# Output projection of the second token tile: one pass over both column halves in place of two

## The chip, the cores and the metric

One core of a Trainium2 chip runs the whole kernel. The metric is the device time of one execution in microseconds (us). Work is spread over five engines that run their own instruction streams and meet at semaphores: TensorE (PE, with its weight loads shown apart as PEld), VectorE (DVE), ScalarE (ACT), GpSimd (POOL) and SyncE (SP), whose queue issues nearly all DMAs here.

## What is computed

One encoder layer on 256 tokens of width 1024, in float32: two attention mixers, gated and merged, one output projection with a residual add, then a top-4-of-32 mixture of experts and a final norm. The change lies between the merged attention and the experts.

```python
def reference(x, norm1_g, w_in, ..., w_o, norm2_g, w_router, b_router, w_gate_up, b_gate_up, w_down, b_down, final_g):
    for l in range(DEPTH):
        ...
        merged = gate_a * (o_a @ w_a_out[l]) + gate_b * (o_b @ w_b_out[l])
        x = x + merged @ w_o[l]
        h2 = rmsnorm(x, norm2_g[l])
        x = x + moe(h2, w_router[l], b_router[l], w_gate_up[l], b_gate_up[l], w_down[l], b_down[l])
    return rmsnorm(x, final_g)
```

`moe` takes the four highest router logits of each token, softmaxes them, sends the token to those experts (`act = (up + 1) * gate * sigmoid(1.702 * gate)`, then `@ w_down`) and sums the weighted results. The experts' weights are 32 x 12 MB, so about 400 of the 434 MB that the kernel reads.

## The kernel before

**Tiles and stages.** The 256 tokens are two tiles of 128 (`t` = 0, 1). The width of 1024 is eight `k` tiles of 128, and results come in two column halves of 512 (`n` = 0, 1), each one PSUM bank. All weights pass through `ring`, 24 slots of 1 MB in SBUF. The front's weights (input projection, attention, `wo`) use slots 0 to 15; slots 16 to 23 are work space of the front until the experts need them. One expert takes 12 slots (8 of `in_up`, 4 of `in_down`), so the ring holds two experts, which the code calls one turn; there are 16 turns, 0 to 15. Turns 0, 1 and 15 are loaded slot by slot (1 MB each, L392), turns 2 to 14 in groups of four slots (4 MB each, L424).

**What lets a load go.** All these loads are issued by SP in program order. The loads of front slots and experts wait on `freed`, a count that PE raises when it has read a slot for the last time. Of turn 0 the loads into slots 7, 8, 9 and 10 wait for the four slots of `wo` (counts 24 to 27), the load into slot 21 is right behind them, the load into slot 22 waits for the router's logits of both tiles (`logit_done`, since it overwrites `x2T`), and that into slot 23 for `sums_opened` and the fourth `h2_ready` (it overwrites `xrow`). Turn 1's load into slot s waits until expert 0 or 1 has used slot s. So SP's queue, around the change, is: slots 7, 8, 9, 10, 21, 22, 23 of turn 0, then turn 1 from slot 0.

**The work around the change**, all of it in an order written out by hand:

- PE: `project(t, k, n)` (L1305) multiplies the merged tile `gateT[:, k, t]` by half n of row tile k of `wo`. Tile 0 runs k outside, n inside. Tile 1 runs all k for n = 0, then all k for n = 1 (L1334 to L1358), with other work placed between: `turn_rows(t, j)` (L1285, four transposes of half j of the new rows of tile t), `route(t, ks)` (L1299, router logits), L1350 (counts), `gather_first` (L1321, gathers tokens for experts 0 and 1). After the second pass come `turn_last_rows` (L1293, the last half in two quarters), the rest of `route(1)`, counts and gathers, and then expert 0 (L1415: up and gate, L1429: down).
- DVE: `residual(t, n)` (L874) adds a projection bank to `xrow`; `take_x2T` (L879) and `take_last_x2T` (L884) copy transposes out; `choose(t)` (L896 to L907) finds the top four of a tile; `normed` (L911) writes `h2`; `first_picks(t)` (L921 to L927) makes the gather masks of experts 0 and 1. `residual(1, 0)` waits for `wo_done` 2, the end of the first pass; `residual(1, 1)` waits for the end of the second.
- ACT: squares for the norm (L626), copies (L636, L631), exponentials (L649), and `take_xT` (L659), the last copy before expert 0.

Counts in the views are of machine instructions: one float32 matmul call of L1305, L1299, L1321, L1415 is two, a transpose is one.

Of the kernel before, what the change touches and what calls it, by code (L numbers as in the profile page):

```python
# [31 lines left out]
SEQ = 256  # L32
TT = SEQ // P
KT = D // P
# [115 lines left out]
def build(nc, x, x_cols, norm2_g, w_router, b_router, b_gate_up, b_down, final_g,  # L150
# [5 lines left out]
    with ExitStack() as ctx:  # L156
# [117 lines left out]
        freed = sem("ring_freed")  # L274
# [18 lines left out]
        wo_done = sem("wo_done")  # L293
        x2_ready, x2_sq, h2_ready = sem("x2_ready"), sem("x2_squares"), sem("h2_ready")
        x2T_ps, x2T_v, x2T_a = sem("x2T_ps"), sem("x2T_vector"), sem("x2T_scalar")
# [33 lines left out]
        def through(name):  # L329

            return FIRST[name] + dict(FRONT)[name]
# [394 lines left out]
        def _(dve):  # L726
# [42 lines left out]
            for t in range(TT):  # L769
                last = dve.tensor_scalar(kr[:, t, :], ps[:, 4 + t, Q_RANK + KV_RANK:LATENT], sums[:, 2 + t:3 + t], None, ALU.mult)  # L770
# [5 lines left out]
            for t in range(TT):  # L776
                dve.tensor_scalar(cn[:, t, 0:Q_RANK], ps[:, 4 + t, 0:Q_RANK], sums[:, 8 + t:9 + t], None, ALU.mult)
                last = dve.tensor_scalar(cn[:, t, Q_RANK:], ps[:, 4 + t, Q_RANK:Q_RANK + KV_RANK], sums[:, 10 + t:11 + t], None, ALU.mult)
# [90 lines left out]
            def residual(t, n, part=slice(0, BANK)):  # L869


                dve.wait_ge(*((wo_done, 1), (wo_done, 1), (wo_done, 2), (freed, through("wo")))[2 * t + n])
                a, z = n * BANK + part.start, n * BANK + part.stop
                dve.tensor_tensor(xrow[:, t, a:z], xrow[:, t, a:z], ps[:, SUM + 2 * t + n, part], ALU.add).then_inc(x2_ready, 1)  # L874

            def take_x2T(t):

                dve.wait_ge(x2T_ps, 2 * t + 1)
                dve.tensor_copy(x2T[:, 0:4, t * P:(t + 1) * P], ps[:, 2 * t, :].rearrange("p (a b) -> p a b", a=4)).then_inc(x2T_v, 1)  # L879
# [29 lines left out]
            def normed(t, n):  # L909
                a = n * BANK  # L910
                dve.scalar_tensor_tensor(out=h2[:, t, a:a + BANK], in0=xrow[:, t, a:a + BANK], scalar=sums[:, 2 + t:3 + t], in1=g2[:, a:a + BANK],  # L911
                                         op0=ALU.mult, op1=ALU.mult).then_inc(h2_ready, 1)
# [20 lines left out]
            dve.wait_ge(x2_sq, 2)  # L933
            mean_square(0).then_inc(ms, 1)
            choose(0)
            residual(1, 0)
            normed(0, 0)
            first_picks(0)
            normed(0, 1)
            take_x2T(1)  # L940
            residual(1, 1, slice(0, SEQ))
            residual(1, 1, slice(SEQ, BANK))
            take_last_x2T(0)
            take_last_x2T(1)
# [86 lines left out]
            with dve.If(any_over > 0):  # L1031
# [4 lines left out]
                with dve.Fori(1, ROUNDS) as r:  # L1036
                    with dve.Fori(0, E) as e:
                        need = dve.value_load(over[0:1, bass.ds(r * E + e, 1)])
                        with dve.If(need > 0):
                            k = dve.snap(done)  # L1040
# [36 lines left out]
        def _(pe):  # L1077
# [202 lines left out]
            def turn_rows(t, j):  # L1280

                pe.wait_ge(x2_ready, 2 * t + j + 1)
                for k in range(4):
                    a = (4 * j + k) * P
                    last = pe.transpose(ps[:, 2 * t + j, k * P:(k + 1) * P], xrow[:, t, a:a + P], ident)  # L1285
                last.then_inc(x2T_ps, 1)

            def turn_last_rows(part):

                pe.wait_ge(x2_ready, 4 + part)  # L1290
                for k in range(2):
                    a = (4 + 2 * part + k) * P
                    last = pe.transpose(ps[:, (MIX, UP)[part], k * P:(k + 1) * P], xrow[:, 1, a:a + P], ident)  # L1293
                last.then_inc(x2T_ps, 1)

            def route(t, ks):

                for k in ks:
                    last = pe.matmul(ps[:, (GATE, Y)[t], 0:E], x2T[:, k, t * P:(t + 1) * P], router_w[:, k, :], start=k == 0, stop=k == KT - 1)  # L1299
                    if k == KT - 1:  # L1300
                        last.then_inc(logit_done, 1)

            def project(t, k, n):
                w = slot(FIRST["wo"] + k // 2, 2, D)
                return pe.matmul(ps[:, SUM + 2 * t + n, :], gateT[:, k, t * P:(t + 1) * P], w[:, k % 2, n * BANK:(n + 1) * BANK],  # L1305
                                 start=k == 0, stop=k == KT - 1)
# [25 lines left out]
            pe.wait_ge(router_ready, 1)  # L1332
            pe.wait_ge(s_const, 16)
            for k in range(KT):  # L1334
                last = project(1, k, 0)
                if k == 3:
                    turn_rows(0, 0)
                    turn_rows(0, 1)
                if k == 5:
                    pe.wait_ge(x2T_v, 1)  # L1340
                    pe.wait_ge(x2T_a, 1)
                    route(0, range(KT))
            last.then_inc(wo_done, 1)
            for k in range(KT):
                last = project(1, k, 1)
                if k % 2:
                    last.then_inc(freed, 1)
                if k == 1:
                    pe.wait_ge(chosen_ready, 1)
                    pe.matmul(ps[:, UP, 0:E], before, chosen[:, 0, :], start=True, stop=True).then_inc(count_done, 1)  # L1350
                if k == 3:
                    turn_rows(1, 0)
                if k == 5:
                    pe.wait_ge(pick_ready, 1)
                    gather_first(0, range(0, 4))
                if k == 6:
                    pe.wait_ge(x2T_v, 2)
                    route(1, range(0, 4))  # L1358

            turn_last_rows(0)  # L1360
            turn_last_rows(1)
            pe.wait_ge(x2T_v, 3)
            route(1, range(4, 6))
            pe.wait_ge(x2T_v, 4)
# [203 lines left out]
```

## Time and profile before

| | us |
|---|---|
| median of three runs | 1132.4 (1130.13 to 1132.68) |
| the profiled execution's own time | 1130.97 |
| its span, first to last instruction | 1129.2 |
| PE busy | 1090.0 (97%) |
| DVE busy | 227.0 (20%) |
| ACT busy | 125.1 (11%) |
| DMA, mean over the span | 386 GB/s |

Times in the views count from the span's start. The stage with the second tile's projection is about 202 to 228 us; expert 0 starts at 228.0 us. The two halves of what follows differ: up to about 645 us PE never waits for a weight, from there on it does once per pair of experts.

### The profile page before, as it was taken

The page shows a single profiled execution, that of the slowest core. Times are in us where ns is not written, and L with a number is a line of the kernel's source. Part 1 is how long each engine was busy: PE and PEld are TensorE (multiplying, and loading weights), DVE is VectorE, ACT ScalarE, POOL GpSimd, SP SyncE. Part 2 cuts the span into 40 slices and gives each one's busy share as a digit, 9 for nine tenths or more (in the row PEclk, how much of TensorE's full clock was granted, in tenths as well). Part 3 has the DMA queues.
Part 4 walks back from the last instruction along what each step waited for, and adds up shares of the span by engine and source line. Part 5 has one row for each costly group of instructions (what it writes and reads, how often), then busy time and mean ns, then how long its engine had stood idle before and what let it go on. Part 6 is the DMA issues. An engine that isn't in the chain of part 4 may idle for free.

```text
span 1129.2 us, 12532 instructions
## 1 busy us (share of the span) xinstructions
PE 1090.0 (97%) x5272; PEld 481.9 (43%) x5273; DVE 227.0 (20%) x563; ACT 125.1 (11%) x271; POOL 29.0 (3%) x43
## 2 busy tenths in 40 slices
PE   8999999999999999999999999999999999999996
PEld 6758887543333333333333433333333333333331
DVE  3174213331111111111112111111111111111112
ACT  1053120210000000000001000000000000000001
POOL 2150000000000000000000000000000000000000
PEclk9999999999999999999999999999999999999999
DMA  9954375499999999999999999999999999999995
GB/s 363 409 221 150 112 270 209 146 423 421 434 431 429 432 430 434 430 431 433 434 430 431 433 434 430 430 434 433 431 430 434 433 431 430 434 431 430 417 421 216
DMA packets 29420, 435.66 MB, mean 386 GB/s; under 512 B 4368, under 2 KB 4624, under 8 KB 7376
## 3 DMA queue, kind: packets, MB, share of 16 engines
q1 hardware_dynamic: 28112, 432.23, 90.8%
q10 hardware_dynamic: 1280, 3.02, 0.8%
q8 instruction: 22, 0.36, 0.1%
q14 instruction: 6, 0.05, 0.0%
HBM read 434.19 MB, written 1.05 MB: 385 GB/s over the span
## 4 chain that ended last, share of the span: by engine, by line
PE 63%; DMA 33%; DVE 2%; issue 0%; SPq 0%; ACT 0%; DVEq 0%; POOL 0%
DMA ring<-in_up 32%; PE ps L1415 26%; PE ps L1429 11%; PE ps L1232 5%; PE ps L1321 3%; PE ps L1437 3%; PE ps L1246 2%; PE ps L1305 2%; PE ps L1115 2%; PE ps L1424 2%; PE ps L1176 1%; DMA ring<-in_front 1%; PE ps L1399 1%; PE ps L1393 1%; PE ps L1140 1%; DVE ring L816 1%
## 5 line engine op out<-in xcount | busy, mean ns | idle before, releaser
L1415 PE MATMUL ps<-ring,work 128*64 128x512 f32 x2048 | 470.9, 605 | 21.7 <-DMA ring<-in_up 21.7
L1415 PEld LDWEIGHTS ps<-ring,work 128*64 128x64 f32 x2048 | 141.8, 138 | 318.8 <-issue 282.6
L1429 PE MATMUL ps<-ring,work 128*64 128x512 f32 x1024 | 226.8, 595 | 1.6 <-DVE work L1025 1.6
L970 DVE TENSOR_SCALAR work<-ps 128x512 f32<-128x512 f32 x32 | 22.1, 692 | 699.7 <-PE ps L1415 699.7
L1429 PEld LDWEIGHTS ps<-ring,work 128*64 128x64 f32 x1024 | 70.7, 137 | 133.6 <-issue 127.9
L1321 PEld LDWEIGHTS ps<-work 128*128 128x128 f32 x512 | 62.1, 191 | 23.9 <-issue 23.2
L1321 PE MATMUL ps<-work 128*128 128x128 f32 x512 | 70.7, 281 | 0.6 <-DVE work L927 0.6
L1437 PE MATMUL ps<-work 64*128 64x512 f32 x264 | 65.6, 615 | 0.7 <-ACT work L682 0.7
L1232 PE MATMUL ps<-work,ring 128*128 128x256 f32 x256 | 56.6, 379 | 0.0
L655 ACT ACTIVATE work<-ps 128x256 f32<-128x256 f32 x33 | 12.7, 384 | 356.2 <-PE ps L1399 356.2
L1232 PEld LDWEIGHTS ps<-work,ring 128*128 128x128 f32 x256 | 48.6, 190 | 6.6
L682 ACT ACTIVATE work<-ps 128x512 f32<-128x512 f32 x32 | 19.1, 597 | 211.9 <-PE ps L1429 211.9
L1437 PEld LDWEIGHTS ps<-work 64*128 64x128 f32 x264 | 22.7, 186 | 43.1 <-issue 41.5
L677 ACT ACTIVATE work<-work 128x512 f32<-128x512 f32 x32 | 20.2, 630 | 163.6 <-DVE work L967 163.6
L1424 PE MATMUL ps<-work 32*64 32x512 f32 x256 | 34.8, 613 | 0.0
L1305 PE MATMUL ps<-ring 128*128 128x512 f32 x64 | 28.8, 596 | 0.0
L659 ACT ACTIVATE work<-ps 128x512 f32<-128x512 f32 x31 | 18.5, 597 | 90.1 <-PE ps L1321 90.1
L1246 PE MATMUL ps<-ring 128*128 128x256 f32 x128 | 28.1, 380 | 0.0
L1115 PE MATMUL ps<-work,ring 128*128 128x256 f32 x128 | 27.8, 379 | 0.0
L1025 DVE COPY work<-ps 128x512 f32<-128x512 f32 x32 | 22.1, 692 | 26.7 <-PE ps L1393 26.7
L530 POOL TENSOR_TENSOR sums<-sums,eps 128x1 f32<-128x1 f32 x4 | 2.2, 554 | 956.3 <-DVE sums L888 956.3
L1115 PEld LDWEIGHTS ps<-work,ring 128*128 128x128 f32 x128 | 24.3, 190 | 3.6 <-issue 0.3
(164 smaller groups left out, 518.7 us busy)
## 6 DMA issues: line engine op xcount, KB each, us to landing
ring<-in_up SPq DMA_DIRECT2D x52, 4096.0 KB, 46.2
ring<-in_down SPq DMA_DIRECT2D x26, 4096.0 KB, 45.0
ring<-in_up SPq DMA_DIRECT2D x48, 1024.0 KB, 11.4
ring<-in_down SPq DMA_DIRECT2D x24, 1024.0 KB, 10.3
ring<-in_front SPq DMA_DIRECT2D x22, 1024.0 KB, 14.7
ring<-in_x SPq DMA_DIRECT2D x2, 512.0 KB, 8.7
ring<-in_x ACTq DMA_DIRECT2D x1, 1024.0 KB, 4.9
out<-ring ACTq DMA_DIRECT2D x4, 256.0 KB, 3.4
```

What stands on the lines that cost most here:

```text
L677: act.activation(sig, gate_c, ACT.Sigmoid, scale=ALPHA).then_inc(sig_ready, 1)
L970: return dve.tensor_scalar(up_c, ps[:, UP, :], LIMIT, -LIMIT, ALU.min, ALU.max)
L1025: dve.tensor_copy(actT, ps[:, MIX, :]).then_inc(actT_ready, 1)
L1115: last = pe.matmul(ps[:, c // 2, c % 2 * SEQ:(c % 2 + 1) * SEQ], w[:, k % 2, c * P:(c + 1) * P], hT[:, k, :], start=k == 0 and c % 2 == 0, ...
L1232: last = pe.matmul(ps[:, 6 + g % 2, c * SEQ:(c + 1) * SEQ], w[:, k, c * P:(c + 1) * P], hT[:, k, :], start=k == 0, stop=k == KT - 1)
L1246: last = pe.matmul(ps[:, d % 4, m * SEQ:(m + 1) * SEQ], w[:, c, d % 4 * P:(d % 4 + 1) * P], oT[:, 4 * m + c, :], start=c == 0, stop=c == 3)
L1305: return pe.matmul(ps[:, SUM + 2 * t + n, :], gateT[:, k, t * P:(t + 1) * P], w[:, k % 2, n * BANK:(n + 1) * BANK], start=k == 0, stop=k = ...
L1321: return pe.matmul(ps[:, bank, q * 2 * CAP:(q + 1) * 2 * CAP], h2[:, t, k * P:(k + 1) * P], pick[:, t, :], start=first, stop=last, skip_gr ...
L1415: last = pe.matmul(ps[n * CAP:(n + 1) * CAP, bank, :], x, w[bank - GATE][:, n * BANK:(n + 1) * BANK], start=k == 0, stop=k == KT - 1, skip ...
L1424: pe.matmul(ps[n * CAP:(n + 1) * CAP, bank, :], expert_row[rows, b, :], up_bias[rows, :], start=False, stop=False, skip_group_check=True)
L1429: last = pe.matmul(ps[n * CAP:(n + 1) * CAP, Y, :], lhs(actT, k), w[:, n * BANK:(n + 1) * BANK], start=k == 0, stop=k == KT - 1, skip_grou ...
L1437: return pe.matmul(ps[:, SUM + n, :], gatedT[rows, b, t, :], y_e[rows, :], start=False, stop=False, skip_group_check=True)
```

## The change

PE: tile 1's projection runs k outside and n inside, like tile 0's, in one pass. `freed` is raised after every second k of that single pass; before, it was after every second k of the second pass. `wo_done` is no longer raised for tile 1. Of the work placed between, `turn_rows(0, ...)` stands behind the fourth of the sixteen calls of `project(1, ...)`, `route(0)` behind the sixth and the count behind the tenth, all three as before; `gather_first(0)` stands behind the fourteenth, as before. What differs is which calls these are. `turn_rows(1, 0)` and `route(1, 0:4)` no longer stand between projections; they come behind the last one.

DVE: `residual(1, 0)` waits for the same event as `residual(1, 1)`, and stands behind `first_picks(0)` and `normed(0, 1)`; the first quarter of `residual(1, 1)` now stands ahead of `take_x2T(1)`.

```diff
@@ DVE
-                dve.wait_ge(*((wo_done, 1), (wo_done, 1), (wo_done, 2), (freed, through("wo")))[2 * t + n])
+                dve.wait_ge(*((wo_done, 1), (freed, through("wo")))[t])
@@ DVE
             choose(0)
-            residual(1, 0)
             normed(0, 0)
             first_picks(0)
             normed(0, 1)
+            residual(1, 0)
+            residual(1, 1, slice(0, SEQ))
             take_x2T(1)
-            residual(1, 1, slice(0, SEQ))
             residual(1, 1, slice(SEQ, BANK))
@@ PE
             for k in range(KT):
-                last = project(1, k, 0)
-                if k == 3:
+                for n in range(2):
+                    last = project(1, k, n)
+                if k % 2:
+                    last.then_inc(freed, 1)
+                if k == 1:
                     turn_rows(0, 0)
                     turn_rows(0, 1)
-                if k == 5:
+                if k == 2:
                     pe.wait_ge(x2T_v, 1)
                     pe.wait_ge(x2T_a, 1)
                     route(0, range(KT))
-            last.then_inc(wo_done, 1)
-            for k in range(KT):
-                last = project(1, k, 1)
-                if k % 2:
-                    last.then_inc(freed, 1)
-                if k == 1:
+                if k == 4:
                     pe.wait_ge(chosen_ready, 1)
                     pe.matmul(ps[:, UP, 0:E], before, chosen[:, 0, :], ...).then_inc(count_done, 1)
-                if k == 3:
-                    turn_rows(1, 0)
-                if k == 5:
+                if k == 6:
                     pe.wait_ge(pick_ready, 1)
                     gather_first(0, range(0, 4))
-                if k == 6:
-                    pe.wait_ge(x2T_v, 2)
-                    route(1, range(0, 4))
-
+
+            turn_rows(1, 0)
             turn_last_rows(0)
             turn_last_rows(1)
+            pe.wait_ge(x2T_v, 2)
+            route(1, range(0, 4))
```

On PE, from the count of tile 0 (L1350) to the counts ahead of expert 0, before:

```order
L1350 MATMUL ps<-work 128x32
L1305 MATMUL ps<-ring 128x512 x2
L1285 MATMUL ps<-const,ring 128x128 x4
L1305 MATMUL ps<-ring 128x512 x2
L1321 MATMUL ps<-work 128x128 x4
L1305 MATMUL ps<-ring 128x512
L1299 MATMUL ps<-work,ring 128x32 x4
L1305 MATMUL ps<-ring 128x512
L1293 MATMUL ps<-const,ring 128x128 x4
L1299 MATMUL ps<-work,ring 128x32 x4
L1321 MATMUL ps<-work 128x128 x4
```

and now (L1348 is the same count):

```order
L1348 MATMUL ps<-work 128x32
L1305 MATMUL ps<-ring 128x512 x4
L1321 MATMUL ps<-work 128x128 x4
L1305 MATMUL ps<-ring 128x512 x2
L1285 MATMUL ps<-const,ring 128x128 x4
L1293 MATMUL ps<-const,ring 128x128 x4
L1299 MATMUL ps<-work,ring 128x32 x8
L1321 MATMUL ps<-work 128x128 x4
```

Four transposes (L1285) and four router calls (L1299) have moved from ahead of the last projection to behind it; the number of calls is the same.

On DVE, from the masks of tile 0 to the norm's sum of tile 1, the difference (- before, + now; `residual(1, 0)`, the L874 of 128x512, stood before this piece, right behind L907 of `choose(0)`):

```order
 L927 TENSOR_SCALAR work<-const,places 128x64 x2
 L911 SCALAR_TENSOR_TENSOR work<-ring,sums,work 128x512
+L874 TENSOR_TENSOR ring<-ring,ps 128x512
+L874 TENSOR_TENSOR ring<-ring,ps 128x256
 L879 COPY ring<-ps 128x4x128
-L874 TENSOR_TENSOR ring<-ring,ps 128x256 x2
+L874 TENSOR_TENSOR ring<-ring,ps 128x256
 L884 COPY ring<-ps 128x2x128 x2
 L888 SCALAR_TENSOR_TENSOR sums<-sums 128x1
```

The residual add of tile 1's first half (128x512) has moved from the middle of the stage to its tail, ahead of the copy L879 that feeds the router, and one quarter of the second half has moved ahead of that copy too.

## Rows read from the trace of the kernel before

**Rows 1.** The page: shares of the chain that ended last, by engine.

```profile
PE 63%; DMA 33%; DVE 2%; issue 0%; SPq 0%; ACT 0%; DVEq 0%; POOL 0%
```

**Rows 2.** The chain that ended last: start us, us, what.

```profile
645.97 48.01 DMA ring<-in_up
...
1074.41 27.72 DMA ring<-in_up
1102.17 1.94 PE ps L1415 x8
```

**Rows 3.** Stretches: busy us (instructions) per engine, PEclk, DMA share, GB/s.

```profile
200.00:205.00 5.00, 5.00 (x13) 2.21 (x12) 1.28 (x2) 1.33 (x4) 0.00 (x0) 1.00 0.00 0
...
215.00:220.00 5.00, 5.00 (x28) 3.44 (x27) 0.69 (x1) 0.00 (x0) 0.00 (x0) 1.00 1.07 385
220.00:225.00 5.00, 4.07 (x28) 2.89 (x26) 3.11 (x13) 3.43 (x8) 0.81 (x2) 1.00 0.91 346
...
260.00:300.00 40.00, 40.00 (x199) 14.23 (x196) 7.58 (x16) 3.22 (x6) 0.00 (x0) 1.00 1.03 428
...
723.00:727.00 4.00, 3.84 (x10) 1.15 (x12) 0.00 (x0) 0.00 (x0) 0.00 (x0) 0.57 1.03 442
```

**Rows 4.** DMA issues on SP's queue in the timeline: start us, us, line.

```profile
213.14 0.33 SPq L392 DMA_DIRECT2D ring<-in_up  x1
...
226.73 0.33 SPq L392 DMA_DIRECT2D ring<-in_down  x1
...
230.00 0.33 SPq L392 DMA_DIRECT2D ring<-in_up  x1
...
250.43 0.33 SPq L392 DMA_DIRECT2D ring<-in_down  x1
...
309.27 0.33 SPq L424 DMA_DIRECT2D ring<-in_down  x1
```

**Rows 5.** Last number: us to landing, for the issues at 213.14, 230.00, 250.43, 309.27.

```profile
ring<-in_up SPq DMA_DIRECT2D x1, 1024.0 KB, 4.7
...
ring<-in_up SPq DMA_DIRECT2D x1, 1024.0 KB, 7.9
...
ring<-in_down SPq DMA_DIRECT2D x1, 1024.0 KB, 7.7
...
ring<-in_down SPq DMA_DIRECT2D x1, 4096.0 KB, 15.6
```

**Rows 6.** PE in order of time: start us, us, line, instructions, idle before.

```profile
205.13 1.04 PE L1285 MATMUL ps<-const,ring 128*128 128x128 f32 x8
...
214.88 0.60 PE L1285 MATMUL ps<-const,ring 128*128 128x128 f32 x4
215.32 1.88 PE L1305 MATMUL ps<-ring 128*128 128x512 f32 x4
...
218.79 0.97 PE L1299 MATMUL ps<-work,ring 128*128 128x32 f32 x8
219.60 1.10 PE L1305 MATMUL ps<-ring 128*128 128x512 f32 x2
221.22 0.77 PE L1293 MATMUL ps<-const,ring 128*128 128x128 f32 x4 [0.51 <-DVE ring L874]
222.17 1.08 PE L1299 MATMUL ps<-work,ring 128*128 128x32 f32 x8 [0.18 <-DVE ring L884]
...
228.02 3.65 PE L1415 MATMUL ps<-ring,work 128*64 128x512 f32 x16
...
723.16 5.30 PE L1415 MATMUL ps<-ring,work 128*64 128x512 f32 x16 [2.15 <-DMA ring<-in_up]
```

**Rows 7.** DVE in order of time: start us, us, line, idle before.

```profile
211.43 0.69 DVE L874 TENSOR_TENSOR ring<-ring,ps 128x512 f32<-128x512 f32 x1 [0.52 <-PE ps L1305]
...
215.52 0.69 DVE L879 COPY ring<-ps 128x512 f32<-128x512 f32 x1 [0.64 <-PE ps L1285]
220.74 0.75 DVE L874 TENSOR_TENSOR ring<-ring,ps 128x256 f32<-128x256 f32 x2 [4.53 <-PE ps L1305]
```

## The prediction

> **What bounds the kernel now.** I read the page's chain first, then the chain in order of time, then stretches, and last the SP queue, PE and DVE around the change. PE is on the chain for 63% and DMA for 33% [rows 1]. In time [rows 2] the long DMA pieces begin at 645.97 us; there are eight, and the last ends at 1102.1, with a weight tile that PE takes at once; what is left behind it is 27 us of fixed work. So the end hangs on when the stream of expert weights arrives, not on PE's work in the front. Now go back: where does that stream start to be continuous? Between 200 and 205 us the DMA moves nothing, and from 260 to 300 its share is 1.03 at 428 GB/s [rows 3]. At 428 GB/s a slot of 1 MB takes 2.45 us. PE frees a slot of expert 0 in half of 3.65 us, about 1.8 (x16 is two up tiles) [rows 6], so once it works on expert 0 it frees faster than the DMA fills, and the stream stays behind PE until PE catches up at 645. Thus **the end moves one for one with the landing of turn 1's first loads**, as long as no later load is issued too late.
>
> What holds that first load? It is issued at 230.00, when PE has read the first slot of expert 0 [rows 4], and lands 7.9 us later, at 237.9. A load on an idle queue, the one at 213.14, takes 4.7 us [rows 5]. The 3.2 us between are the queue: slots 7 to 10, 21, 22 and 23 of turn 0 are ahead, and they could not go before 213.14, since the DMA idled until then for want of a freed slot.
>
> **What the change does to the queue.** The first `freed` of `wo` came after the tenth projection call of tile 1, and comes now after the fourth. The work up to the fourth call is unchanged, so that is 205.3 us (the transposes behind it start at 205.13 [rows 6]). The load into slot 7 goes 7.8 us earlier and runs where the DMA is idle. Call 8 is at about 211.3, call 12 at about 215.0 as before, call 16 at 219.45 (below). Slots 10 and 21 are issued together then and land by 219.45 + 4.7 + 2.45 = 226.6. Slot 22 goes with the router's logits at about 224.3 and lands at the later of 229.0 and 226.6 + 2.45, so 229.1. Slot 23 is issued at 226.73 now [rows 4], later by the shift of the tail s, and lands at about 232.4. A load issued at 230.00 + s then finds the queue empty: all 3.2 us of lag are gone, and what remains is s.
>
> **What the change does to PE's tail.** Before, the last projection ends at 219.60 + 1.10 = 220.70 [rows 6]. Four transposes (215.32 - 214.88 = 0.44 us) and four router calls (219.60 - 218.79 = 0.81 us) leave the stretch ahead of it, nothing enters, and the sixteen calls cost the same in either order; so it ends at 219.45, 1.25 earlier. Behind it the chain is longer, with 0.04 us from one engine to the next (220.70 to 220.74 [rows 6, 7]):
> - L874, 128x512, 0.69 us [rows 7]: 219.49 to 220.18;
> - four transposes L1285, 0.60 [rows 6]: to 220.82;
> - copy L879, 0.69 [rows 7]: to 221.55. The first quarter of the add fits in DVE's wait for the transposes and costs nothing;
> - last quarter of the add, half of 0.75 [rows 7]: to 221.93.
>
> Before, the adds ended at 220.74 + 0.75 = 221.49 and the router's logits at 222.17 + 1.08 = 223.25, 1.76 later. Now eight calls stand behind the add instead of four, +0.81, and they cover PE's wait of 0.18 for L884 [rows 6]. Logits: 221.93 + 1.76 + 0.81 - 0.18 = 224.3. So **s = +1.0 us**. All that follows (choice of experts, masks, gathers, expert 0 at 228.02) hangs on the logits by the same steps and moves by s: expert 0 starts at about 229.0. Its bounds: 0.4, if the four router calls hide wholly behind DVE and the hand-overs are no longer than before; 1.8, if each of four new hand-overs costs 0.18 like the one shown.
>
> Edits that I cost at nothing: `residual(1, 0)` leaves the middle of DVE's order, where DVE had waits of 0.5 us and more; the masks of tile 0 come no later, and PE needs them only behind call 14. ACT's first square of tile 1 moves to the tail, but its last one starts only when the last add ends, 0.4 later than before, and PE's logits are 1.0 later, so the norm's factor stays covered.
>
> **The sum.** Turn 1's first load: issued at 231.0, landed at 231.0 + 4.7 = 235.7 instead of 237.9, 2.2 us earlier. One later load is nearer to its limit: slot 8, the first that expert 0's down tiles free, is issued at 250.43 and lands 7.7 later, at 258.1 [rows 4, 5]. Now it is issued at 251.4 and can't land before 256.1: 2.0 us earlier, though the seven in front of it would allow 2.2. Turn 2's third group, issued at 309.27 and landed at 324.9, is next: unqueued it needs about 4.7 + 3 x 2.45 = 12.1 us (my estimate from the rows of 1 MB), so 310.3 + 12.1 = 322.4, 2.5 earlier than before; not a limit. So the stream and the end come **2.0 us earlier**. On the profiled execution's own time that is 1130.97 - 2.0 = 1129.0; the median of the runs stands 1.4 above that execution, so for a median 1132.4 - 2.0 = **1130.4**. With s at its bounds the saving is 2.6 to 1.2.
>
> For the price of an unqueued load there is also the Trainium skill, DMA: Bandwidth & Descriptors, section "Anatomy of one DMA": a fit, made on the GpSimd path, of 2.0 us plus the bytes at 436 GB/s. By it 1 MB takes an estimated 4.4 us where this trace has 4.7, and 4 MB 11.6; with those the saving would be 2.3.
>
> **Rivals.**
> 1. **The lag is mostly an accident.** From 215 to 225 the DMA moved 385 and 346 GB/s with a share of 1.07 and 0.91, not 428 [rows 3]. That is (43 + 82) x 5 / 428 = 1.5 us of the 3.2. If the slow packets come in other executions less, the queue there is only 1.7 long and the change saves 0.7 - 0.2 = 0.5: 1131.9. If they come at a restart of the queue, the new order has more restarts, and one in front of slot 23 gives the same. For it: the runs differ by 2.5 us among themselves. Against: nothing shows that they are random.
> 2. **PE paces the stream, and it ends slower.** If the groups of 4 MB are not behind but just in time, the stream follows PE's frees, and all moves later by s. The place is turn 2's third group: 15.6 us from issue to landing [rows 5]. If an unqueued 4 MB load takes that long, the end is 1.0 later: 1133.4 on the median. The point from which it decides is 15.6 - 1.0 = 14.6 us; the DMA's full share from 260 to 300 and my 12.1 speak against.
> 3. **PE's clock falls in the tail.** PE now has two waits of nearly 1 us there (219.45 to 220.2, then for the last quarter of the add). The trace shows the granted clock at 0.57 of full in the mean from 723 to 727 [rows 3], where it fell to its lower level, 1.2 GHz, and the two up tiles there took 5.30 us instead of 3.65, after a wait of 2.15 [rows 6]. At expert 0's start this costs 1.65 us and leaves 0.35 of the saving: 1132.0 to 1132.1. Against it: from 220 to 225 PE is idle for 0.93 of 5 us, at full clock [rows 3]. The Trainium skill, TensorE: Matmul & The Clock Gate, section "HAM oscillation", says that waits for data re-throttle TensorE; by that rule the time would be this rival's, and the trace agrees only for the longer wait.
> 4. **More than the lag comes back.** The sum can't give over 3.2. A saving above 3.4 needs s near zero and a stream that also runs more evenly, or a median that stands nearer to the profiled execution than before: 1128.5.
>
> **How the numbers follow.** Forecast (1129.5 to 1131.2) 0.56; rival 1 0.18; rival 2 0.08; rival 3 0.06; rival 4 0.12. The range takes in rival 1 and 3, rival 2 to 1133.4 at the top, and 1130.97 - 3.0 = 1128.0 at the bottom. What a measurement of this kernel can tell from no change is about 0.3%, 3.4 us. The forecast, rivals 1 and 3 and all of rival 2's price lie within it; rival 4 and some of the forecast's lower edge lie below: faster 0.16, same 0.79, slower 0.05 for a rival 2 with a long s.
>
> **What would show it.** Right: the first 1 MB issue of this stage at about 205.4 and one each at about 211.4 and 215.1; the last L1305 ending near 219.5; L896 of tile 1 near 224.4; expert 0 near 229.0; the turn 1 issue near 231.0 landing in 4.7 to 5 us; the 1 MB issue near 251.4 landing in under 5.5. The last L1415 after a DMA wait, and the span, 2.0 earlier. Wrong: a landing time of that issue still near 7 us (rival 1), 4 MB landings following their issues at a fixed distance (rival 2), a granted clock under 1.00 between 220 and 232 (rival 3), or an expert 0 that starts over 1.8 us later.

## The result, and the profile after

The changed kernel takes 1135.13 us (median of 12 executions, 1131.91 to 1138.23); the kernel before, on the same chips, takes 1132.11 (12 executions, 1129.26 to 1134.49). The ratio is 1.0028 with a 95% interval of 1.0015 to 1.0041: 3.0 us slower, where 2.0 us faster was forecast. The executions of the changed kernel differ in the mean granted clock of TensorE: three at 0.987 to 0.989 took 1131.9 to 1133.8 us (median 1132.35), nine at 0.982 to 0.986 took 1135.0 to 1138.2 (median 1135.6). (In one experiment below, e2_fill_late, two of twelve executions were disturbed, at 1255 and 2199 us, and its figures are those of the other ten.)

Its profiled execution is one of the nine: 1135.17 us, with a span of 1133.4, against 1130.97 and 1129.2. Its page and its chain, to be read beside [rows 1, 2]:

```profile
PE 66%; DMA 31%; DVE 2%; issue 0%; SPq 0%; ACT 0%; DVEq 0%; POOL 0%
```

```profile
649.94 48.09 DMA ring<-in_up
...
1107.13 1.87 PE ps L1411 x8
```

The first long DMA piece begins 3.97 us later than before, and the span is 4.2 longer. Behind 650 us two small differences nearly cancel. The last weight tile is taken 4.96 later and not 3.97, after one more fall of PE's clock near 1048 us, where two up tiles took 5.03 us instead of 3.65; and 0.7 comes back behind the last add. So most of the loss stands in front of 650 us, and is looked for between the edit, at 205 us, and the landings of the second turn.

One thing first. The two executions don't reach the edited place at the same time. DVE's first add of tile 0 is work that the edit leaves alone, and it starts at 202.00 before and at 201.30 after (start us, us, engine, line, tiles; first before, then after):

```profile
202.00 1.28 DVE L874 TENSOR_TENSOR ring<-ring,ps 128x512 f32<-128x512 f32 x2 [12.68 <-PE ps L1305]
```

```profile
201.30 1.29 DVE L874 TENSOR_TENSOR ring<-ring,ps 128x512 f32<-128x512 f32 x2 [12.68 <-PE ps L1305]
```

Over the traces of all kernels here this **anchor** lies between 201.26 and 205.14. That is as much as the whole effect, so I compare moments by their distance from the anchor, and say so where I do. The traces also show what goes with it. In the seven with an anchor of 202.0 or less TensorE's granted clock is 1.00 from 12 to 24 us; in five (e2, e4, e5, e8, e9: 202.9 to 203.95) it was at its lower level for 3.4 us near 15 us, and in e1 (205.14) for 6.8. The stretch from 12 to 24 us, before and then e1:

```profile
12.00:24.00 12.00, 10.48 (x38) 6.63 (x37) 5.56 (x18) 2.12 (x11) 1.87 (x3) 1.00 1.01 418
```

```profile
12.00:24.00 12.00, 8.77 (x20) 4.79 (x21) 3.06 (x10) 0.88 (x4) 1.38 (x2) 0.72 1.01 417
```

Now SP's loads. The timeline of the changed kernel (start us, us, line), and under it how long the issues at 204.63, 233.98, 235.69, 254.40 and 293.34 took to land (last number); they answer to [rows 4, 5]:

```profile
204.63 0.33 SPq L392 DMA_DIRECT2D ring<-in_up  x1
210.72 18.30 SPq L392 DMA_DIRECT2D ring<-in_down  x6
233.98 0.33 SPq L392 DMA_DIRECT2D ring<-in_up  x1
...
293.34 0.35 SPq L424 DMA_DIRECT2D ring<-in_up  x1
```

```profile
ring<-in_up SPq DMA_DIRECT2D x1, 1024.0 KB, 4.7
...
ring<-in_up SPq DMA_DIRECT2D x1, 1024.0 KB, 4.7
...
ring<-in_up SPq DMA_DIRECT2D x1, 1024.0 KB, 6.5
...
ring<-in_down SPq DMA_DIRECT2D x1, 1024.0 KB, 6.7
...
ring<-in_up SPq DMA_DIRECT2D x1, 4096.0 KB, 15.7
```

Slot 7's load goes as early as it was meant to, and turn 1's first load finds an empty queue: 4.7 us instead of 7.9. But it is issued at 233.98, 32.68 behind the anchor, where before it was 28.00 behind: **4.68 us later, not 1.0**. The reason stands on PE. Here is PE in the changed kernel around that place (idle time before, in brackets):

```profile
216.79 1.88 PE L1305 MATMUL ps<-ring 128*128 128x512 f32 x4
219.46 0.66 PE L1285 MATMUL ps<-const,ring 128*128 128x128 f32 x4 [0.78 <-DVE ring L874]
219.95 0.38 PE L1293 MATMUL ps<-const,ring 128*128 128x128 f32 x2
221.22 0.44 PE L1293 MATMUL ps<-const,ring 128*128 128x128 f32 x2 [0.89 <-DVE ring L874]
221.50 2.92 PE L1299 MATMUL ps<-work,ring 128*128 128x32 f32 x16
224.23 2.05 PE L1321 MATMUL ps<-work 128*128 128x128 f32 x8
...
228.01 3.79 PE L1321 MATMUL ps<-work 128*128 128x128 f32 x16 [0.17 <-DVE work L927]
231.72 3.93 PE L1411 MATMUL ps<-ring,work 128*64 128x512 f32 x16
```

And the stretch from 222 to 232, with busy us (instructions) of PE, PEld, DVE, ACT and POOL, the granted clock, the DMA share and GB/s; before, then after:

```profile
222.00:232.00 10.00, 9.01 (x60) 5.98 (x60) 7.07 (x36) 4.73 (x10) 0.81 (x2) 1.00 0.99 394
```

```profile
222.00:232.00 10.00, 9.82 (x47) 9.47 (x48) 4.48 (x25) 4.52 (x8) 0.81 (x2) 0.50 0.85 314
```

The last projections end at 218.67. Then PE waits 0.78 us for the add and 0.89 for its last quarter. At 222.1 the granted clock falls to 0.50, which is 1.2 GHz, and stays there for 10.2 us. PE is busier than before and does less: 47 instructions in 9.82 us instead of 60 in 9.01.

### The profile page after: what moved, and what is told of

It is laid out like the page before. It is cut to its first block, busy times and chain, and to the rows that moved or that the text cites. A ratio compares the mean times of both kernels' runs of the same rounds, so it can differ in the third digit from the quotient of the medians.

```text
span 1133.4 us, 12532 instructions
## 1 busy us (share of the span) xinstructions
PE 1095.9 (97%) x5272; PEld 486.7 (43%) x5273; DVE 226.8 (20%) x563; ACT 125.5 (11%) x271; POOL 28.9 (3%) x43
## 4 chain that ended last, share of the span: by engine, by line
PE 66%; DMA 31%; DVE 2%; issue 0%; SPq 0%; ACT 0%; DVEq 0%; POOL 0%
DMA ring<-in_up 30%; PE ps L1411 28%; PE ps L1425 11%; PE ps L1232 5%; PE ps L1321 3%; PE ps L1433 3%; PE ps L1246 2%; PE ps L1305 2%; PE ps L1115 2%; PE ps L1420 2%; PE ps L1176 1%; PE ps L1395 1%; DMA ring<-in_front 1%; PE ps L1389 1%; PE ps L1140 1%; DVE ring L816 1%
## 5 line engine op out<-in xcount | busy, mean ns | idle before, releaser
L1321 PEld LDWEIGHTS ps<-work 128*128 128x128 f32 x512 | 64.6, 198 | 23.5 <-issue 23.2
L1321 PE MATMUL ps<-work 128*128 128x128 f32 x512 | 73.3, 288 | 0.2 <-DVE work L927 0.2
L1433 PE MATMUL ps<-work 64*128 64x512 f32 x264 | 65.6, 615 | 0.7 <-ACT work L682 0.7
L1246 PE MATMUL ps<-ring 128*128 128x256 f32 x128 | 28.1, 380 | 0.0
L1115 PE MATMUL ps<-work,ring 128*128 128x256 f32 x128 | 27.8, 379 | 0.0
L1025 DVE COPY work<-ps 128x512 f32<-128x512 f32 x32 | 22.1, 692 | 26.7 <-PE ps L1389 26.7
```

Source lines behind the costliest of these rows:

```text
L1025: dve.tensor_copy(actT, ps[:, MIX, :]).then_inc(actT_ready, 1)
L1115: last = pe.matmul(ps[:, c // 2, c % 2 * SEQ:(c % 2 + 1) * SEQ], w[:, k % 2, c * P:(c + 1) * P], hT[:, k, :], start=k == 0 and c % 2 == 0, ...
L1246: last = pe.matmul(ps[:, d % 4, m * SEQ:(m + 1) * SEQ], w[:, c, d % 4 * P:(d % 4 + 1) * P], oT[:, 4 * m + c, :], start=c == 0, stop=c == 3)
L1321: return pe.matmul(ps[:, bank, q * 2 * CAP:(q + 1) * 2 * CAP], h2[:, t, k * P:(k + 1) * P], pick[:, t, :], start=first, stop=last, skip_gr ...
L1433: return pe.matmul(ps[:, SUM + n, :], gatedT[rows, b, t, :], y_e[rows, :], start=False, stop=False, skip_group_check=True)
```

## The experiments

Two things could carry the loss. The **clock** theory: the two new waits let the clock fall, and that delays expert 0. The **queue** theory: the earlier loads, or the emptier queue behind them, change how the stream of weights runs. And the forecast's gain of 3.2 us in the queue had gone somewhere. Each experiment's time is the median of its executions; the kernel before, run beside them, had medians of 1131.84 to 1132.26. The ratios compare with it and carry the verdict; they differ by up to 0.0006 from the ratios of these medians. Each trace is of one execution.

### The waits filled, the loads left as in the change

Three matmuls of a constant into unused space of PSUM stand in each of the two waits:

```diff
+            for _ in range(3):
+                pe.matmul(ps[:, Y, 0:P], ident, ident, start=True, stop=True)
             turn_rows(1, 0)
             turn_last_rows(0)
+            for _ in range(3):
+                pe.matmul(ps[:, UP, P:2 * P], ident, ident, start=True, stop=True)
             turn_last_rows(1)
```

> The changed kernel plus six small matmuls of 128x128 on PE in its two new waits: three between the last projection and the transposes of tile 1 (the wait of 0.78 us), three between the two halves of turn_last_rows (the wait of 0.89 us). They write free columns of two PSUM banks and change no result. Theory 1 (the clock): the changed kernel's TensorE clock fell from 222 to 232 us because PE stood idle in these waits; with them filled the clock stays at 1.00, expert 0 starts about 3.4 us earlier than in the changed kernel (near 228.5 to 229 us on the trace), and the time is 3 us below it, about 1131 to 1132. Theory 2 (the lower clock comes from what PE does there, transposes and 32-column matmuls, not from the waits): the clock falls as before, time as the changed kernel, about 1135.

Measured: 1133.10 us (1130.49 to 1135.89), ratio 1.0002 [0.9990, 1.0014]. PE in its trace, and the stretch from 222 to 232:

```profile
222.35 0.83 PE L1354 MATMUL ps<-const 128*128 128x128 f32 x6
223.29 0.66 PE L1285 MATMUL ps<-const,ring 128*128 128x128 f32 x4
...
224.00 0.83 PE L1358 MATMUL ps<-const 128*128 128x128 f32 x6
225.06 0.44 PE L1293 MATMUL ps<-const,ring 128*128 128x128 f32 x2 [0.22 <-DVE ring L874]
```

```profile
222.00:232.00 10.00, 8.85 (x72) 7.89 (x70) 6.91 (x29) 6.52 (x13) 0.81 (x2) 1.00 0.89 332
```

The clock stays at 1.00, and turn 1's first load is issued 28.81 us behind the anchor. That is 0.81 later than before: the longer chain by itself, which I had put at 1.0. Against the 4.68 of the change it leaves 3.87 for the clock. (This execution was the slowest of the twelve, 1135.89 us; its anchor is 3.1 us later than that of before.)

The same with the first filler alone, and with the second alone (the first, or the last, two added lines above):

> The changed kernel with the three filler matmuls in the first new wait alone (before the transposes of tile 1). The wait of 0.89 us between the halves of turn_last_rows stays. If the two waits together lower the clock: level with e1_fill, about 1133. If the second wait is the one that counts: the clock at 0.50 near 225 to 235 us in the trace and about 1135.

> The changed kernel with the three filler matmuls in the second new wait alone. If the two waits together lower the clock: level with e1_fill, about 1133. If the first wait is the one that counts: the clock falls and about 1135.

Measured: 1132.40 us (1130.82 to 1134.04), ratio 1.0003 [0.9992, 1.0014], and 1132.14 (1128.78 to 1136.04), ratio 1.0004 [0.9990, 1.0018]. With the first filler all ten executions have a mean clock of 0.988 to 0.990; with the second, eight of ten do better than 0.986, and the other two took 1135.94 and 1136.04. In both profiles the clock is 1.00 in the tail, with the other wait still there (`e10_fill_first`). That alone proves little, since the next experiment shows a trace in which the clock holds through both waits; it is the executions together that carry it.

```profile
218.51 0.83 PE L1354 MATMUL ps<-const 128*128 128x128 f32 x6
219.45 0.66 PE L1285 MATMUL ps<-const,ring 128*128 128x128 f32 x4
...
221.22 0.44 PE L1293 MATMUL ps<-const,ring 128*128 128x128 f32 x2 [0.89 <-DVE ring L874]
221.49 1.87 PE L1299 MATMUL ps<-work,ring 128*128 128x32 f32 x16
```

So it is the two waits together that matter; breaking one is enough, or nearly. Around the two waits stand eight transposes, and no run put other work in their place, so whether they have a part in it is not shown.

### The loads late, the waits left as in the change

Here SP holds slots 7 to 10 back until the count, so that they go when they went before; PE's order is the new one:

```diff
+            sp.wait_ge(count_done, 1)
             after_front(range(7, 11))
```

> The changed kernel with the loads into slots 7 to 10 held until the count of tile 0, and nothing else: the fourth corner beside the changed kernel, e1_fill and e2_fill_late. Theory (two separate causes): the clock falls as in the changed kernel, since PE's waits are the same, and the queue ahead of turn 1 is worth nothing either way: 1135 (1134 to 1136). If early loads were the harm in the changed kernel: about 1133.

Measured: 1135.15 us (1130.33 to 1139.85), ratio 1.0026 [1.0009, 1.0043]; the changed kernel has 1135.13. **The earlier loads, for whose sake the queue gets empty, show no gain** here. This pair by itself leaves about 2 us to each side; the pairs e1 and e2, e5 and e6 below narrow that. Of its twelve executions five have a clock of 0.988 to 0.991 and took 1130.3 to 1133.1; seven have 0.982 to 0.985 and took 1135.1 to 1139.9. Its profiled execution is one of the five, with the same two waits:

```profile
222.11 0.66 PE L1286 MATMUL ps<-const,ring 128*128 128x128 f32 x4 [0.78 <-DVE ring L875]
...
223.87 0.44 PE L1294 MATMUL ps<-const,ring 128*128 128x128 f32 x2 [0.89 <-DVE ring L875]
224.15 1.87 PE L1300 MATMUL ps<-work,ring 128*128 128x32 f32 x16
225.85 1.14 PE L1322 MATMUL ps<-work 128*128 128x128 f32 x8
...
228.80 2.05 PE L1322 MATMUL ps<-work 128*128 128x128 f32 x16 [0.58 <-DVE work L928]
230.78 3.65 PE L1412 MATMUL ps<-ring,work 128*64 128x512 f32 x16
```

This gives the price of the clock line by line, since the instructions are the same as in the rows of after. Counted from the first transpose L1285 (L1286 here), the router's calls start 2.04 us later in both. The eight gather calls start at +4.77 against +3.74, the sixteen at +8.55 against +6.69, expert 0's up tiles at +12.26 against +8.67, and turn 1's load goes at +14.52 against +10.65. These are 1.03, 1.86, 3.59 and 3.87 us: every small step between the logits and the experts pays, not the two tiles of expert 0 alone.

### Both

> As e1_fill, and SP waits for the count of tile 0 (raised at about 213 us) before the load into slot 7, so the loads into slots 7 to 10 go as late as in the kernel before and the queue stands full at turn 1's first load. Theory A, the prediction's (each us of queue ahead of turn 1's first load is a us at the end): slower than e1_fill by about 2 us. Theory B (a load that reaches an empty queue pays for it with slow first packets, and with full queues that price is paid behind earlier loads, so the queue costs nothing in the end): within 1 us of e1_fill.

Measured: 1131.8 us (1129.91 to 1132.71, ten executions), ratio 0.9990 [0.9977, 1.0002]. With e1, e9 and the change this makes a square:

| | loads early | loads late |
|---|---|---|
| waits open | 1135.13 | 1135.15 |
| waits filled | 1133.10 | 1131.8 |

The waits are worth 2.0 and 3.4 us; the loads 0.0 and, the wrong way round for the forecast, 1.3. The intervals are about 1.4 us to each side, so that 1.3 is not clear of nothing; but a gain of 2.0 from early loads is excluded in this pair.

### The wait in the old order

This is the kernel before with four copies on DVE between the last projection and the last adds, so that PE waits there, and nothing moved:

```diff
+            dve.wait_ge(freed, through("wo"))
+            for _ in range(4):
+                stepped(dve.tensor_copy(places[:, :, E:3 * E], slots.unsqueeze(1).to_broadcast([P, TT, CAP])))
+                step_wait()
             residual(1, 1, slice(0, SEQ))
```

> The kernel before with four extra DVE copies (about 0.25 us each) between the end of the last projection and residual(1, 1), so that PE waits about 1 us longer there, in the old order of work. Theory 1: the clock falls to 0.50 here too, some us behind the wait, the matmuls up to expert 0 take twice as long, and expert 0 starts 3 us or more later than before (231 us or later). Theory 2: the clock stays at 1.00 and expert 0 starts 1.0 us later, at 229. By the prediction's rule the end follows expert 0's start.

Measured: 1134.18 us (1132.68 to 1139.33, 8 executions), ratio 1.0024 [1.0005, 1.0042]. PE, and the stretch from 222 to 234:

```profile
223.31 1.02 PE L1297 MATMUL ps<-const,ring 128*128 128x128 f32 x4 [1.56 <-DVE ring L874]
...
225.99 2.05 PE L1325 MATMUL ps<-work 128*128 128x128 f32 x8
```

```profile
222.00:234.00 12.00, 10.52 (x46) 9.47 (x48) 6.90 (x32) 5.31 (x10) 0.81 (x2) 0.57 0.99 378
```

A wait of 1.56 us makes the clock fall in the old order too, at 223.7 and again for 10.2 us, and the eight gather calls take the same 2.05 us as in the change. So a wait brings the fall without the new order, and e1 kept the clock with the new order: the cause is the idle time and not the order of the projections. Turn 1's load goes 32.61 behind the anchor, almost the number of the change (32.68). The fall is not in every execution here either, to judge by the mean clock: three of eight are at 0.981 to 0.983 and took 1136.8 to 1139.3 us, five at 0.986 to 0.990 took 1132.7 to 1134.3.

### A longer queue in front of turn 1

The kernel before with slots 7 to 10 held until the last add:

```diff
+            sp.wait_ge(x2_ready, 4)
             after_front(range(7, 11))
```

> The kernel before with the loads into slots 7 to 10 held until the first quarter of residual(1, 1) is added, about 221.2 us instead of 213.1: nothing on PE changes, only the queue in front of turn 1 is 8 us longer. If the end follows the landing of turn 1's first load one for one, as the prediction has it: 8 us slower, about 1140. If PE's start of expert 0 paces the stream, no change.

Measured: 1139.03 us (1137.44 to 1139.97, 4 executions), ratio 1.0068 [1.0054, 1.0083], 7.2 us more. SP's rows, and the landing of the load at 230.89:

```profile
222.08 0.33 SPq L392 DMA_DIRECT2D ring<-in_up  x1
222.45 5.49 SPq L392 DMA_DIRECT2D ring<-in_down  x6
230.89 0.33 SPq L392 DMA_DIRECT2D ring<-in_up  x1
```

```profile
ring<-in_up SPq DMA_DIRECT2D x1, 1024.0 KB, 13.3
```

Here the load of turn 1 is issued where it was before (28.01 behind the anchor), and lands 5.4 later than before's 7.9. From issue to the landing of turn 2's first group of 4 MB it takes 81.4 us instead of 75.1, so 6.3 later. A longer queue costs about what it is long (5.4, 6.3 and, in the median of only four executions, 7.2, where 8 was expected); a shorter one gives nothing back.

### What became of the 3.2 us

The distances behind turn 1's first issue, in us, from the traces. Each slot is 1 MB; slot 8 is issued at 20.4 in all of these, turn 2's first group at 59.4:

| | slot 0 lands | slot 1 | slot 8 | slot 14 | slot 23 | turn 2's first group |
|---|---|---|---|---|---|---|
| before | 7.9 | 10.4 | 28.1 | 43.0 | 65.4 | 75.1 |
| after | 4.7 | 8.2 | 27.1 | 42.8 | 65.2 | 75.1 |
| e10_fill_first | 4.7 | 8.4 | 26.7 | 42.8 | 65.2 | 75.0 |
| e1_fill | 4.8 | 8.5 | 27.8 | 42.9 | 65.8 | 75.5 |
| e9_late | 6.2 | 9.1 | 27.5 | 43.3 | 65.6 | 75.4 |
| e2_fill_late | 7.3 | 9.8 | 27.7 | 42.7 | 65.0 | 74.7 |
| e8_before_later | 13.3 | 15.8 | 34.3 | 49.3 | 71.7 | 81.4 |

In the row of before the slots land 2.48 us apart, with one step of 2.8 (slot 6). In the row of after slot 1 lands 3.5 behind slot 0, slot 6 3.6 behind slot 5, and by slot 14 all but 0.2 of the gain of 3.2 is gone. The bytes don't flow at the full rate there. The stretches from 234 to 246 and from 258 to 270 before, the first of them after, and both in e1:

```profile
234.00:246.00 12.00, 12.00 (x58) 3.50 (x54) 2.38 (x4) 1.01 (x2) 0.00 (x0) 1.00 1.01 425
...
258.00:270.00 12.00, 12.00 (x62) 3.69 (x60) 0.00 (x0) 0.38 (x1) 0.00 (x0) 1.00 1.01 421
```

```profile
234.00:246.00 12.00, 12.00 (x60) 3.58 (x56) 1.83 (x10) 0.77 (x2) 0.00 (x0) 1.00 0.91 335
```

```profile
234.00:246.00 12.00, 12.00 (x60) 3.60 (x56) 2.09 (x12) 0.77 (x2) 0.00 (x0) 1.00 0.98 369
...
258.00:270.00 12.00, 12.00 (x58) 3.92 (x54) 0.00 (x0) 0.60 (x1) 0.00 (x0) 1.00 0.98 383
```

In e1 from 258 to 270 the share is 0.98 and the rate 383 GB/s; the kernel before has 421 with 1.01. The engines are nearly as busy and move less, so the packets take longer. The trace shows one more thing: a load is spread over 16 DMA engines, and in the steady stream of before the last of them finishes 2.2 to 2.4 us behind the first. On a load that finds the queue empty the first and the last are 0.4 apart (after, slot 0), then 1.5 (slot 1), and 2.3 from slot 14 on. As that distance grows, the landing, which is that of the last engine, comes later. That is some 1.9 us of the 3.2. It fits what is seen, but e8 has slots 0 to 3 only 0.4 to 0.5 apart too, in a queue that is never short, and also a step of 3.7 to slot 4. So what spreads the engines, and what takes the rest, stays open.

One run asked whether a fuller queue keeps the stream even: a needless load of 0.5 MB behind slot 22, with the gather and the filler of e5 below.

```diff
             expert_load(0, 22)
+            sp.wait_ge(loaded[11], 32)
+            sp.dma_start(ring[:, 11:12, 0:F], unit(0, 2)[:, :, 3 * SLOT:3 * SLOT + F]).then_inc(again, 16)
...
+                    if static and e == 0:
+                        pe.wait_ge(again, 16)
```

> e5_gather_fill with one needless load of 0.5 MB (a half of slot 11 again, same bytes) behind the load into slot 22, so that the stream does not run dry between slots 22, 23 and turn 1. By the prediction's rule this adds up to 1.2 us to the queue and so to the end. By the restart theory turn 1's first load lands about 1 us later but the 23 behind it take 57.5 us in place of about 61, and the end comes 2 us earlier than in e5_gather_fill.

Measured: 1132.11 us (1130.12 to 1133.27), ratio 1.0002 [0.9993, 1.0011]. Turn 1's first load takes 6.6 us, and turn 2's first group lands 75.7 behind its issue. Lag or no lag, it is the same 75 once more. The restart theory has its first half (the first landing 1.9 us later than the 4.7 of e5); the 23 slots behind it take 59.4 us instead of the 60.1 of e5, not 57.5.

### The gather in the first wait

Here useful work fills the first wait: the gather of tile 0's picks (`if k == 6`) is moved to it.

```diff
-                if k == 6:
-                    pe.wait_ge(pick_ready, 1)
-                    gather_first(0, range(0, 4))
...
+            pe.wait_ge(pick_ready, 1)
+            gather_first(0, range(0, 4))
             turn_rows(1, 0)
```

> The changed kernel with gather_first(0, 0:4), four calls, moved from behind the fourteenth projection call into the first new wait, ahead of turn_rows(1, 0). Work in the place of fillers: the last projection ends 0.89 us earlier, the tail starts 0.8 us earlier, and the first wait is filled. Theory 1 (clock by waits): if filling one of the two waits is enough, the clock stays at 1.00, expert 0 starts at about 228 us and the time is 1130 to 1131; if the second wait alone lowers the clock, the gain is only the 0.8 us: about 1134. Theory 2 (clock by kind of work): falls as before, about 1134.

> e3_gather_tail (four gather calls in the first new wait) plus three 128x128 filler matmuls in the second. Clock theory: no fall of the clock in any execution; against e3_gather_tail, whose second wait may still lower the clock in some executions, up to 0.5 us faster; expert 0 starts about 15.0 us behind the count of tile 0, as in the kernel before (15.1). If the queue of loads in front of turn 1 cost what the prediction says, this kernel would be 2 to 3 us faster than before, 1129 to 1130. If the slow restart of the stream gives that back, it is level with before, 1131.5 to 1132.5.

> e5_gather_fill with the loads into slots 7 to 10 held until the count of tile 0, so they go as in the kernel before. The prediction's theory (queue ahead of turn 1 costs): 2 us slower than e5_gather_fill. Restart theory (a load behind an empty queue is in step on all 16 DMA engines and the next loads pay 2 to 4 us until they are out of step; with a queue this is paid before turn 1): equal to e5_gather_fill or up to 1 us faster, turn 1's loads evenly spaced at 2.48 us from the first.

Measured: 1133.04 us (1131.88 to 1137.03), ratio 1.0007 [0.9994, 1.0020]; with the second filler added (e5) 1133.15, 1.0006 [0.9994, 1.0019]; with the late loads besides (e6) 1132.61, 1.0012 [1.0002, 1.0022]. The 1130 to 1131 expected of e3 did not come, and e5 and e6 are level within about 1.3 us: early loads give nothing like 2 us here either, and the even spacing expected of e6 has steps of 3.1 and 4.2. In e3 the issue is 27.92 behind the anchor, so all of the longer chain is won back, and turn 2's first group lands 75.5 behind it: the time is that of the kernel before and not 2 us under it. In the profiles of e5 and e6 the clock fell for 3.4 us near 227 and 225, with waits of no more than 0.6 us in front, though e5 was expected to be free of it. Why it fell there, and not in e1 or e10, I can't say. No version tried is faster than the kernel before by more than its interval.

## Why the prediction was wrong, point by point

- **The bound.** Right in the main: the end follows the landings of the second turn (DMA piece +3.97, span +4.2), and PE's work in the front counts only through them.
- **The load of slot 7.** Right: predicted 205.3, 211.3 and 215.0; issued at 204.63, 210.72 and 214.38, in an execution whose anchor is 0.70 earlier.
- **The tail at full clock.** Right: the last projection was to end at 219.45 and ended at 218.67 + 0.70 = 219.4; s was put at 1.0 (0.4 to 1.8) and is 0.81 in e1, e9, e10 and e11.
- **The lag.** Right as far as it goes: 4.7 us to landing, all 3.2 gone.
- **"The end moves one for one with the landing of turn 1's first loads."** This is the first of two steps that failed, and it would have made the forecast wrong even with a steady clock: e1, e10 and e11 took 1132.1 to 1133.1, where 1129.5 to 1131.2 was forecast. I took spacing at 2.45 us per slot from the steady stream, and checked later loads only against the 4.7 of an unqueued one: slot 8 was to land under 5.5 us behind its issue, and took 6.7. From first issue to turn 2's first group it is 74.7 to 76.4 us in all kernels whose first load took 4.7 to 7.9. One for one holds, roughly, only when the queue grows (e8). The saving of 2.0 was therefore a loss of 0.8: the issue later by s, and nothing back. Rival 1 had half of this, that slow packets come at a restart and eat the gain; it priced that at 1131.9 and named it an accident of [rows 3].
- **Rival 2.** Its sign is there: turn 2's first group of 4 MB lands 15.3 to 16.1 us behind its issue in the kernels before, after, e1 to e5 and e9 to e11 (16.4 in e7, 17.1 in e6, 22.0 in e8), the third group, which it named, in 15.7 after as in 15.6 before, and at a steady clock all moves later by s, as it said. Its reason, a stream that waits for PE's frees, doesn't fit the kernel before, whose DMA share is 1.01 with 421 to 425 GB/s in the stretches above. But I have no load of 4 MB on an empty queue, so my 12.1 us for one was never shown, and I can't exclude that some floor of that kind adds to the slow packets.
- **Rival 3, the clock.** This is the second step that failed: the forecast's sum has no term for the clock, and it is what took the time out of the range. The rival had the mechanism and the place; its chance of 0.06 and its price of 1.65 were both wrong. I argued that PE was idle for 0.93 of 5 us at full clock before, and that the fall that I had looked at came after a wait of 2.15. But no row of before showed two waits so close (1.67 us of idle time within 2.6), and nothing in it said which side of 2.15 such a pair is on. Nor does a wait's length decide alone: the trace of before has eight waits of 2.14 or 2.15 us for a weight, and the clock fell behind five of them and not behind those that end at 694.02 (the first row below), 781.44 and 1044.86. So full clock in one place of one execution was weak evidence. The price counted expert 0's two up tiles; the router's calls, the gathers and the count stand on the same path and slowed down too. It measured 3.87.

```profile
694.02 3.65 PE L1415 MATMUL ps<-ring,work 128*64 128x512 f32 x16 [2.14 <-DMA ring<-in_up]
...
723.16 5.30 PE L1415 MATMUL ps<-ring,work 128*64 128x512 f32 x16 [2.15 <-DMA ring<-in_up]
```

- **The sum, redone for the two traces.** From the anchor: chain +0.81, clock +3.87, lag -3.2, slower spacing +3.2, the rest of the program +0.2 (+1.0 up to the last weights, -0.1 to the last add and -0.7 behind it); together +4.9. The anchor is 0.7 earlier: +4.2, the difference of the spans. The median moved by 3.0 and not by 4.2, most likely since the clock doesn't fall in every execution: by the mean clock nine of twelve here and seven of twelve in e9. That count is an estimate, as the mean also holds what happens elsewhere: the traces of e1 and e2 have a mean of 0.986 and yet 1.00 throughout this stage, since the clock fell near 15 us instead, and the kernel before, run 93 times beside the experiments, is at 0.986 or under 14 times (median 1133.9, the others 1131.8). The three executions of the change with the better clock have 1132.35, 0.5 above those others, about the s of 0.81.
- **The range** (1128.0 to 1133.4) missed by 1.7 us, because the two failures were never added: no gain in the queue, and the clock. At a steady clock it would have stayed inside, by the 1133.1 of e1.

The Trainium skill, TensorE: Matmul & The Clock Gate, section "HAM oscillation", describes a loop in which PE waits for the next DMA and TensorE is throttled again by it; I set it aside since the trace agreed only for the longer wait. The trace of after goes the same way, with two waits of 0.78 and 0.89 us, and those are waits for DVE and not for a DMA.

## What to carry to other kernels

When a reorder puts PE's waits close together, ask first for the clock: look at all the waits of the stretch and not only at the longest, give a fall a real chance where no trace shows such a pair at full clock, and take as its cost everything on the path behind it until the clock is back. A few needless matmuls in one of the waits are a cheap trial. And before you count a shorter queue as gain, compare the distance from the first issue to a late landing between kernels with different lags; where it is constant, the queue was not what bounded.

## What the runs showed that I had not expected

- Two waits of 0.78 and 0.89 us, 1.7 us apart by their starts, took TensorE to 1.2 GHz for 10.2 us, at a price of 3.87; and not every time (the same order of work on PE kept 2.4 GHz in the profiled execution of e9). What decides between executions stays open.
- Behind an empty queue the first 1 MB lands after 4.7 us and the second 3.5 us later, against 2.48 in a running stream; the DMA then moves 335 to 383 GB/s at a share of 0.91 to 0.98.
- The start of one and the same instruction, 200 us into the kernel, differed by up to 3.88 us (201.26 to 205.14) between profiled executions, with nothing edited ahead of it. The order of these starts is that of how long the clock was low near 15 us: not at all, 3.4 us, or 6.8.
